# Inverting the chunk matrices on 32x32 diagonal blocks, stored 32 columns wide

## The reference, cut to what matters

```python
w_log = -jax.nn.softplus(-(w0 + jnp.tanh(wl) @ w2)) - 0.5
decay = jnp.exp(-jnp.exp(w_log))
vec_a = -kk                       # kk: unit length in each head
vec_b = kk * a_h
def step(S, inp):
    r_t, w_t, k_t, v_t, a_t, b_t = inp
    sa = jnp.einsum('bhij,bhj->bhi', S, a_t)
    S = S * w_t[:, :, None, :] + sa[..., None] * b_t[:, :, None, :] + v_t[..., None] * k_t[:, :, None, :]
    return S, jnp.einsum('bhij,bhj->bhi', S, r_t)
```

## Time and profile before

| | us |
|---|---|
| median of 3 runs | 1974.87 |
| the profiled execution's own time | 1975.43 |
| its span (first to last instruction) | 1973.9 |
| TensorE busy | 1895.1 (96%) |
| VectorE busy | 1136.9 (58%) |
| ScalarE busy | 707.8 (36%) |
| one pair of the pair loop, by the distance between two pairs | 54.9 |

### The profile page before, as it was taken

One profiled execution on the slowest core, in us unless ns is written; L12 is line 12 of the kernel. 1 busy time (PEld: TensorE's weight loads), 2 busy tenths in 40 slices (PEclk: granted clock), 3 DMA queues, 4 the chain that ended last, 5 costly groups with the idle time before them and its releaser, 6 DMA issues.

```text
span 1973.9 us, 40799 instructions
## 1 busy us (share of the span) xinstructions
PE 1895.1 (96%) x16568; PEld 1805.6 (91%) x16568; DVE 1136.9 (58%) x1994; ACT 707.8 (36%) x926; POOL 168.1 (9%) x126
## 2 busy tenths in 40 slices
PE   5999899999999999998999999999999999999997
PEld 3999769998888888888999899999999999999997
DVE  5333865225777777666655566666666666344444
ACT  4333243433344333334334333333333333233332
POOL 2600334431000000000000000000000000000000
PEclk7999999989999999999999999999999999999998
DMA  4644323432222222225445544444444544554443
GB/s 182 220 160 170 115 70 129 125 120 73 79 100 100 82 98 100 75 93 197 158 162 170 190 167 170 162 159 168 163 158 168 170 160 163 189 166 161 162 164 131
DMA packets 50458, 283.61 MB, mean 144 GB/s; under 512 B 7072, under 2 KB 12128, under 8 KB 24288
## 3 DMA queue, kind: packets, MB, share of 16 engines
q1 hardware_dynamic: 43488, 261.00, 38.8%
q10 hardware_dynamic: 2784, 12.63, 1.7%
q0 software_dynamic: 4128, 9.18, 1.3%
HBM read 274.51 MB, written 8.27 MB: 143 GB/s over the span
## 4 chain that ended last, share of the span: by engine, by line
PE 83%; DVE 10%; ACT 2%; issue 2%; DMA 1%; POOL 1%; DVEq 0%; ACTq 0%; SPq 0%
PE bank L558 25%; PE bank L560 23%; PE bank L559 23%; PE bank L840 3%; DVE w_lo L507 1%; PE bank L879 1%; POOL w_lo L507 1%; DVE w_lo L515 1%; DVE squares_k L1704 1%; DVE x_raw L1506 1%; ACT w_hi L523 1%; DVE rope_tmp L1544 1%; PE bank L699 1%; DMA conv_params<-in_conv_params 1%; PE bank L539 1%
## 5 line engine op out<-in xcount | busy, mean ns | idle before, releaser
L558 PE MATMUL bank<-x_split,w_lo 128*128 128x288 f32 x2944 | 907.4, 308 | 33.1 <-DVE x_split L1512 17.2
L559 PE MATMUL bank<-x_split,w_hi 128*128 128x288 f32 x2944 | 873.3, 297 | 0.0
L560 PE MATMUL bank<-x_split,w_hi 128*128 128x288 f32 x2944 | 870.7, 296 | 0.0
L523 ACT ACTIVATE w_hi<-w_raw 128x2048 fp32r<-128x2048 f32 (+1 forms) x264 | 472.6, 1790 | 589.4 <-PE bank L560 581.6
L507 DVE TENSOR_TENSOR w_lo<-w_raw,w_hi 128x2048 fp32r<-128x2048 f32 (+1 forms) x215 | 451.0, 2098 | 310.7 <-ACT w_hi L523 310.7
L558 PEld LDWEIGHTS bank<-x_split,w_lo 128*128 128x128 f32 x2944 | 556.8, 189 | 60.4 <-issue 35.8
L559 PEld LDWEIGHTS bank<-x_split,w_hi 128*128 128x128 f32 x2944 | 557.9, 190 | 4.1 <-issue 0.7
L560 PEld LDWEIGHTS bank<-x_split,w_hi 128*128 128x128 f32 x2944 | 558.7, 190 | 0.0
L558 PE MATMUL bank<-act_split,w_lo 128*128 128x288 f32 x704 | 209.2, 297 | 3.0 <-DVE w_lo L507 3.0
L559 PE MATMUL bank<-act_split,w_hi 128*128 128x288 f32 x704 | 208.4, 296 | 0.0
L560 PE MATMUL bank<-act_split,w_hi 128*128 128x288 f32 x704 | 207.7, 295 | 0.0
(11 more groups left out here) (363 smaller groups left out, 1711.2 us busy)
## 6 DMA issues: line engine op xcount, KB each, us to landing
w_raw<-in_w_up SPq DMA_DIRECT2D x88, 1024.0 KB, 4.9
w_raw<-in_w_in SPq DMA_DIRECT2D x48, 1024.0 KB, 5.0
w_raw<-in_w_down SPq DMA_DIRECT2D x64, 704.0 KB, 4.1
w_raw<-in_w_gate SPq DMA_DIRECT2D x32, 1024.0 KB, 4.9
w_raw<-in_w_p SPq DMA_DIRECT2D x16, 1024.0 KB, 4.9
w_raw<-in_w_o SPq DMA_DIRECT2D x16, 1024.0 KB, 4.9
x_raw<-in_x SPq DMA_DIRECT2D x4, 576.0 KB, 6.7
h<-in_x ACTq DMA_DIRECT2D x1, 2304.0 KB, 9.0
```

Of the source, the lines that this page charges most:

```text
L523: actv(WHI[:, slot, 0:kt], WRAW[:, slot, 0:kt], ACT.Copy).then_inc(sem("w_hi"), 1)
L558: mm(out, wl, hi, start=first and k == ks[0], stop=False, skip_group_check=True)
L559: mm(out, w, lo, start=False, stop=False, skip_group_check=True)
L560: ins = mm(out, w, hi, start=False, stop=last and k == ks[-1], skip_group_check=True)
```

## The change

**Inverse.** U1, L1, U2, L2 and the inverse while it grows (now `TB`) hold only the diagonal 32x32 blocks: 128 partitions are four row groups of 32 (par and block b within the chunk), and each of the four u takes 32 columns instead of 64. `four` runs over four row groups with K = M = N = 32: sixteen matmuls of 32x32x32 where there were eight of 64x64x64. The last merge, which joins two 32x32 blocks to a 64x64 matrix, multiplies only the blocks that matter (eight matmuls each for its second and third group), and its result is copied into the off-diagonal block of `TT` on 32 partitions at a time. The diagonal blocks of TT are filled before by a multiplication of TB with a 0/1 mask (`own_block`), one new VectorE instruction. The mask m64l and its multiplication (L1794) are gone. All copies of bank 2 and bank 3 in the inverse have 128 columns instead of 256. Halves l1_end, u2_end, l2_end only keep the memory layout.

**Products.** b.a is now computed on 32x32 diagonal blocks (16 matmuls, K = 64), b.r apart from it (8 of 64x64), and k.a with k.r as before (8 of 64x128). a.b is computed as 16 matmuls of diagonal blocks, and 8 of 64 rows by the first 32 columns, for the last merge.

**Decay.** The triangular constant has a zero column ahead of each chunk (65 columns a chunk, 5 a request), so one product in bank 7 holds the exclusive sums as the inclusive ones moved by a column. The matmuls into bank 2 and the third exponential are gone; `head` reads the two views, which now are runs of 64 in rows of 65.

The constants loaded at the start shrink from 1256 to 1042 columns.

```diff
+BL = 32
+DEC = NCH * (CH + 1) + DB * (DS + 1)
@@ constants
+    tri = np.zeros((P, 2, CH + 1))
+    tri[:, :, 1:] = ((blk(CH) & upi) * (0.5 * DECAY_SCALE)).reshape(P, 2, CH)
...
+    own = np.zeros((P, 2, BL))
+    own[i, i // BL % 2] = 1.0
+    c["own_block"] = own.reshape(P, -1)
@@ TensorE: log_decay
-                for bank, tri, tris in ((7, tri_incl, tris_incl), (2, tri_excl, tris_excl)):
-                    for tt in range(2):
-                        mm(BK[bank][:, tt * P:(tt + 1) * P], LDT[:, tt, :], tri, start=True, stop=True)
-                    ins = mm(BK[bank][:, SEQ:N], LDT[0:NS, 2, :], tris, start=True, stop=True)
-                ins.then_inc(sem("log_decay"), 1)
+                for tt in range(2):
+                    w = 2 * (CH + 1)
+                    mm(BK[7][:, tt * w:(tt + 1) * w], LDT[:, tt, :], tri, start=True, stop=True)
+                mm(BK[7][:, NCH * (CH + 1):DEC], LDT[0:NS, 2, :], tri_s, start=True, stop=True).then_inc(sem("log_decay"), 1)
@@ TensorE: pair, the products
-                for x, src in enumerate((BT, KTL)):
-                    for tt, par in chunks:
-                        c0 = (2 * tt + par) * CH
+                for tt, par in chunks:
+                    for b in range(2):
+                        c0, q = (2 * tt + par) * CH + b * BL, slice((2 * par + b) * BL, (2 * par + b + 1) * BL)
                         for e, h in enumerate(halves):
-                            ins = mm(BK[5 + e][halves[par], x * SEQ + tt * P:x * SEQ + (tt + 1) * P], src[h, c0:c0 + CH],
-                                     AR[h, :, c0:c0 + CH], start=True, stop=True)
+                            mm(BK[5 + e][q, tt * P:tt * P + BL], BT[h, c0:c0 + BL], AR[h, 0, c0:c0 + BL], start=True, stop=True)
+                for tt, par in chunks:
+                    c0 = (2 * tt + par) * CH
+                    for e, h in enumerate(halves):
+                        mm(BK[5 + e][halves[par], tt * P + CH:(tt + 1) * P], BT[h, c0:c0 + CH], AR[h, 1, c0:c0 + CH],
+                           start=True, stop=True)
+                for tt, par in chunks:
+                    c0 = (2 * tt + par) * CH
+                    for e, h in enumerate(halves):
+                        ins = mm(BK[5 + e][halves[par], SEQ + tt * P:SEQ + (tt + 1) * P], KTL[h, c0:c0 + CH],
+                                 AR[h, :, c0:c0 + CH], start=True, stop=True)
...
                 for tt, par in chunks:
+                    for b in range(2):
+                        c0, q = (2 * tt + par) * CH + b * BL, slice((2 * par + b) * BL, (2 * par + b + 1) * BL)
+                        for e, h in enumerate(halves):
+                            mm(BK[(4, 7)[e]][q, tt * BL:(tt + 1) * BL], AR[h, 0, c0:c0 + BL], BT[h, c0:c0 + BL], start=True, stop=True)
+                for tt, par in chunks:
                     c0 = (2 * tt + par) * CH
                     for e, h in enumerate(halves):
-                        mm(BK[(4, 7)[e]][halves[par], tt * CH:(tt + 1) * CH], AR[h, 0, c0:c0 + CH], BT[h, c0:c0 + CH],
+                        mm(BK[(4, 7)[e]][halves[par], (2 + tt) * BL:(3 + tt) * BL], AR[h, 0, c0:c0 + CH], BT[h, c0:c0 + BL],
                            start=True, stop=True)
@@ TensorE: pair, the inverse
+                quads = [slice(g * BL, (g + 1) * BL) for g in range(4)]
                 def four(bank, c0, lhs, rhs):
                     for u in range(4):
-                        for r in halves:
-                            ins = mm(BK[bank][r, c0 + u * CH:c0 + (u + 1) * CH], lhs[r, u], rhs[r, u], start=True, stop=True)
+                        for q in quads:
+                            ins = mm(BK[bank][q, c0 + u * BL:c0 + (u + 1) * BL], lhs[q, u], rhs[q, u], start=True, stop=True)
...
-                        for r in halves:
-                            mm(BK[2][r, u * CH:(u + 1) * CH], TT[r, u], ident[r, r], start=True, stop=True)
-                    four(3, 256, U1, TT).then_inc(sem("inv_mm"), 1)
+                        for q in quads:
+                            mm(BK[2][q, u * BL:(u + 1) * BL], TB[q, u], ident[q, q], start=True, stop=True)
+                    if merge == 0:
+                        four(3, 256, U1, TB).then_inc(sem("inv_mm"), 1)
+                    else:
+                        for u in range(4):
+                            for g in (1, 3):
+                                ins = mm(BK[3][quads[g - 1], 256 + u * BL:256 + (u + 1) * BL], ML[quads[g], u // 2, 1, u % 2, :],
+                                         TB[quads[g], u], start=True, stop=True)
...
-                        four(3, 0, L1, L2).then_inc(sem("inv_mm"), 1)
+                        for u in range(4):
+                            for g in (0, 2):
+                                ins = mm(BK[3][quads[g], u * BL:(u + 1) * BL], L1[quads[g], u], L2[quads[g], u], start=True,
+                                         stop=True)
@@ ScalarE
-                actv(PEXP[:, 0, :], BK[7][:, 0:N], ACT.Exp)
-                actv(PEXP[:, 1, :], BK[7][:, 0:N], ACT.Exp, scale=-1.0)
-                actv(PEXP[:, 2, :], BK[2][:, 0:N], ACT.Exp).then_inc(sem("decay"), 1)
+                actv(PEXP[:, 0, :], BK[7][:, 0:DEC], ACT.Exp)
+                actv(PEXP[:, 1, :], BK[7][:, 0:DEC], ACT.Exp, scale=-1.0).then_inc(sem("decay"), 1)
...
-                    actv(flat(dst[:]), BK[2][:, 0:256], ACT.Copy).then_inc(sem("inv_u"), 1)
+                    actv(flat(dst[:]), BK[2][:, 0:4 * BL], ACT.Copy).then_inc(sem("inv_u"), 1)
@@ VectorE: pair
-                    ins = V.tensor_tensor(U1[:, 2 * e:2 * e + 2, :], src[:, 0:2, 0:CH], spread(m16u, 1, [P, 2, CH]), ALU.mult)
+                    ins = V.tensor_tensor(U1[:, 2 * e:2 * e + 2, :], src[:, 0:2, 0:BL], spread(m16u, 1, [P, 2, BL]), ALU.mult)
...
-                V.tensor_copy(L2[:], grid(3, 256)).then_inc(sem("inv_l"), 1)
+                V.tensor_copy(L2[:], blocks(3, 256)).then_inc(sem("inv_l"), 1)
...
-                V.tensor_tensor(U1[:], ML[:], spread(m64l, 1, [P, 4, CH]), ALU.mult)
...
                 add_t(3, 0, 6)
+                st.mark(V.tensor_tensor(TT[:].rearrange("p u (k f) -> p u k f", k=2), spread(TB[:], 2, [P, 4, 2, BL]),
+                                        spread(own_block, 1, [P, 4, 2, BL]), ALU.mult))
...
-                add_t(3, 0, 8)
+                st.sync()
+                for q in (slice(0, BL), slice(2 * BL, 3 * BL)):
+                    ins = V.tensor_copy(TT[q, :, BL:CH], BK[3][q, 0:4 * BL].rearrange("p (u f) -> p u f", u=4))
+                ins.then_inc(sem("inv_l"), 1)
```

More of the change, by code:

```diff
@@ L109, in constants @@
     small[s, 2 * NS:3 * NS] = (b4 & low)[s, s]
-    small[s, 3 * NS:4 * NS] = (b4 & upi)[s, s] * (0.5 * DECAY_SCALE)
-    small[s, 4 * NS:5 * NS] = (b4 & up)[s, s] * (0.5 * DECAY_SCALE)
-    small[both, 5 * NS:] = np.arange(2 * NS)[:, None] % NS // DS == np.arange(DB)[None, :]
+    for b in range(DB):
+        small[s, 3 * NS + 5 * b + 1:3 * NS + 5 * b + 5] = (b4 & upi)[s, DS * b:DS * b + DS] * (0.5 * DECAY_SCALE)
+    small[both, 3 * NS + 5 * DB:] = np.arange(2 * NS)[:, None] % NS // DS == np.arange(DB)[None, :]
     c["small"] = small
@@ L168 @@
 ATT_STEPS = [("sample", 0), (0, 0), (0, 1), (1, 0), (1, 1), ("sample", 1)]
-PAIR_STEPS = 14
+PAIR_STEPS = 15
 UP_STEPS = 6
@@ L328, in build @@
     inv_at = m.at
[L329 to L333, removed]
+    U1 = m("u1", [P, 4, BL])
+    TB = m("t_blocks", [P, 4, BL])
+    L1 = m("l1", [P, 4, BL])
+    m("l1_end", [P, 4, BL])
+    U2 = m("u2", [P, 4, BL])
+    m("u2_end", [P, 4, BL])
+    L2 = m("l2", [P, 4, BL])
+    m("l2_end", [P, 4, BL])
+    ML = m("m_low", [P, 2, 2, 2, BL])
     TT = m("t_inv", [P, 4, CH])
@@ L396, in build @@
     ident, mean_ones, head_ones = cst("ident"), cst("mean_ones"), cst("head_ones")
-    tri_incl, tri_excl = cst("tri_incl"), cst("tri_excl")
-    eye_ch, m_ab, m16u, m16l, m32l, m64l = (cst(x) for x in ("eye_ch", "m_ab", "m16u", "m16l", "m32l", "m64l"))
+    tri = cst("tri")
+    eye_ch, m_ab, eye_bl, m16u, m16l, m32l = (cst(x) for x in ("eye_ch", "m_ab", "eye_bl", "m16u", "m16l", "m32l"))
+    own_block = cst("own_block").rearrange("p (k f) -> p k f", k=2)
     small = cst("small", NS)
     ms_ab, ms_l = small[:, 0:2 * NS], small[:, 2 * NS:3 * NS]
-    tris_incl, tris_excl = small[:, 3 * NS:4 * NS], small[:, 4 * NS:5 * NS]
-    ms_req = cst("small", 2 * NS)[:, 5 * NS:5 * NS + DB]
+    tri_s = small[:, 3 * NS:3 * NS + 5 * DB]
+    ms_req = cst("small", 2 * NS)[:, 3 * NS + 5 * DB:3 * NS + 6 * DB]
     h_spill = nc.dram_tensor("h_spill", [P, KT * N], F32, kind="Internal").ap()
@@ L853, in pair @@
                 four(3, 0, U2, L2)
-                four(3, 256, L2, TT).then_inc(sem("inv_mm"), 1)
+                four(3, 256, L2, TB).then_inc(sem("inv_mm"), 1)
                 fill(3)
@@ L859, in pair @@
                 four(2, 0, U1, L1)
-                four(3, 256, L1, TT).then_inc(sem("inv_mm"), 1)
+                four(3, 256, L1, TB).then_inc(sem("inv_mm"), 1)
```

(16 more changed lines are left out.)

53 lines of the change are left out of this document (28 added, 25 removed).

## The result

| | median us | runs | against the kernel before (95%) |
|---|---|---|---|
| before | 1975.29 | 4 | |
| changed | 2002.29 | 4 | 1.0146 [1.0107, 1.0186] |

The changed kernel is slower by about 27 us; 1952.0 had been forecast, 23 us faster. Its profiled execution took 1999.96 us with a span of 1998.4. Its pairs stand 57.1 to 61.8 us apart, where they stood 54.9 and were to stand 52.1.

The account below looks back on a forecast made before the run. TensorE was taken to bound a pair's first half, VectorE the second. Eight pairs at -2.8 us (-22.4) and -0.5 at the start made -22.9, forecasting 1952.0 us; range 1946 to 1958 (72%), wider range 1945 to 1966.

Parts of the forecast that it names:

- the sum: Per pair: -3.4 + 0.6 - 0.1 = -2.9 us, less 0.1 for something unseen: -2.8; eight pairs -22.4.
- cover: TensorE fills between steps of the inverse, expected to hide VectorE's and ScalarE's work; if one is gone, 0.2 to 0.7 us a pair.
- for something I have not seen: Allowance in the sum per pair: 0.1 us taken off the expected gain of 2.9.
- Overlap of two only: Rival: only two array parts work at once, so a group stays at 0.48 us; 1981 us, chance 8%.
- no overlap in a bank: Rival: a group's 32 records, all writing one bank, don't overlap; 2035 us; 5% together with a floor near 25 ns.
- The floor of 25 ns between starts: Skill's rule that matmuls start no closer than about 25 ns: 0.8 us a group, slower pair; 5% with no overlap.
- (1): Inverse: 14 groups each go from 0.47 to 0.24 us by overlap of four array parts; -3.4 us a pair.
- (2): Products of a, b, k, r: more records and changes of shape, about 1.9 us; +0.6 us a pair.
- (3): Changes of matmul shape inside the inverse: one more ahead of L866, one less ahead of L894 and L922; -0.1 us.
- (4): log_decay loses one of two parts: 0 in the loop, w_lo wait 0.4 to about 1.4 us; -0.5 us in all.
- (5): VectorE in the second half, views in rows of 65 or 5: 0, bounds -0.1 to +0.5 us.
- (6): VectorE and ScalarE between the steps of the inverse stay hidden by the fills: 0; otherwise 0.2 to 0.7 us a pair.

Follow-up runs that it names:

- run 3: Kernel before, with the 8 products of a and b given 9 times in each pair (1780 instructions): 2016.57 us, 1.0214 of the kernel before.
- run 4: Kernel before, with the 8 products of a and b given 17 times in each pair (2036 instructions): 2041.03 us, 1.0344 of the kernel before.
- run 10: Changed kernel with the shortened body, its 8 products of b and r given nine times (1892 instructions): 1994.23 us, 1.0107 of the kernel before.
- run 5: Kernel before, with the products of a and b given five times in each pair (1652 instructions): 1979.88 us, 1.0021 of the kernel before.
- run 8: Changed kernel with some fills and state matmuls left out of TensorE's loop (1706 instructions): 1959.63 us; kernel before with the same left out: 1972.39 us.
- run 9: Changed kernel, same result, with VectorE transposes replacing some TensorE groups and two groups joined (1636 instructions): 1945.22 us, 0.9840 of the kernel before.
- run 6: Kernel before with only the change's edits of log_decay, exponentials and VectorE's views, nothing of the inverse: 1976.38 us, 1.0006 of the kernel before.
- run 1: Changed kernel with TensorE's loop over seven pairs written out, no backward branch: 1971.76 us, 0.9991 of the kernel before.

## Why the prediction was wrong

**The step that failed is the sum: it has no term for loading the loop's instructions.** Each term was a time of TensorE's array or of a cover, the 0.1 "for something I have not seen" was all that stood for the rest, and the place that the instructions need was put at nothing without a reason. I wrote that the price of the change is a matter of records per time; it is also a matter of records per pass. The change adds 250 records of matmul and as many weight loads, 500 instructions, to a loop of 1524, and that takes it over a limit between 1652 and 1780, with 1706 at its edge. The forecast's 52.1 us a pair became 59.3 in the mean of six. The waits show where most of the 7.2 us lie: pauses at L850 (14.1 us in six passes, 2.3 each), pauses at L574, L575 and L871 (13.2 us, 2.2 a pass), and a gate at L574 that comes late (1.1 us each of six times). I put the gate down to the branch ahead of it without a run for that alone; the wait stands in runs 3, 4 and 10 too, which load anew, and in none that doesn't. The 3.3 us of the branch themselves fall into the stretch that VectorE bounds and are paid only in part; how much of the 7.2 is the branch and how much the lower clock, no run separates. That the loss goes when the code fits and comes back when it doesn't is shown by runs 3, 5 and 8 to 10.

No rival had it either. "Overlap of two only" (1981) and "no overlap in a bank" (2035) would have been right in sign for the wrong reason: the groups are 0.27 us apart, and all records of a group share one bank. The floor of 25 ns between starts, from the Trainium skill's "TensorE: Matmul & The Clock Gate", is contradicted by 8.4 ns here.

**Point by point.** (1) The inverse: in the undisturbed pair of run 8 the chain gives its pieces 3.37 + 0.73 + 0.26 + 0.37 = 4.7 us against 7.76, -3.0 where I had -3.4. A group that stands alone takes 0.27, near the 0.24; where two or three follow each other they take 0.32 each (10 ns a record, not 7.5). The mechanism held, its size was 12% off: overlap on four row groups in one bank, which no row of before had shown, was an extrapolation, and it held. (2) The products: 0.29 + 0.40 + 0.44 + 0.36 + 0.37 = 1.86 us, forecast 1.9: right. (3) Not visible by itself. (4) log_decay: nothing in the loop, right (run 6), but the slack came out elsewhere: TensorE's wait for w_lo did not grow to 1.4, it waits 0.8 us a pair for squares_k at L800 instead, ahead of the fill that needs w_lo. Run 6, with the decay part alone, has the same wait. (5) VectorE's second half: 18.6 us from L775 to the end of w_lo in run 1, 18.5 before by the same measure: 0, right. (6) The covers held: no wait on a t_blocks or l copy shows in any run with the code in place.

Where it could have been seen ahead: the branch's row of before (0.21 us), the 7 packets of the instruction queue from 450 to 850 us, neither of which the prediction used, and the number of instructions between two branches before and after the change. The two rows say that the code stays in place, the number that it grows by a third. Where the limit lies they don't say: that took runs 3, 5 and 8.

## What to carry to other kernels

A hardware loop has a size. Before small matmuls are split into smaller ones in a loop, count the engine's instructions between two backward branches, and look at the branch's duration and at the packets of the instruction queue: a branch of 0.2 us and next to no packets mean that the code stays in place. Here a loop of TensorE ran from place up to 1652 instructions and was loaded anew in every pass from 1780 on, at a cost of 5 to 7 us a pass; the way back was to take out instructions whose result another engine can make, not to write the loop out.

## What the runs showed of the hardware that I had not expected

- The limit is sharp. 1636 and 1652 instructions: no reload. 1706: two passes of six reload, the others don't. 1780, 1892, 2024, 2036: every pass, 9 to 10 packets of 16 KB each. No run moves the start of a loop against the blocks in which code is loaded, so whether the limit depends on that is open. The Trainium skill has 2048 instructions for TensorE ("Runtime: NRT & Kernel Launch", section Instruction fetch mechanics) and, in "Advanced Engine Details and Errata", section ISA Cache, lines of 16 KB with 256 instructions, but "Only 2 cache lines!". What a loop could use here is less than 2048 and more than two lines: 1780 instructions are 6.95 lines, and they did not stay; 1652 are 6.45, and they did.
- Even code in a straight line can be outrun. In run 1 the dense stretch of small matmuls pauses twice a pair, 0.6 us each; packets come no closer together than 3.35 us, and where they are under 5 us apart, TensorE goes through some 230 instructions from one to the next.
- 32x32 matmuls on four diagonal parts of the array overlap in one bank: 8.4 ns a record in a group alone, 10 ns in longer runs, where one part by itself takes 30 (L868).
- VectorE transposes four 32x32 blocks on each of four partition groups in 0.30 us, little more than a copy of the same size (0.28).
